# Index queries and keys held as high and low fp32r parts, their scores as three products on the two row halves

## The chip, the cores and the metric

The kernel runs on one core of one Trainium2 chip. The metric is the device time in microseconds (us) of one execution; the time before the change is the median of three runs. TensorE is PE in the profile (PEld are its weight loads), VectorE is DVE, ScalarE is ACT, GpSimd is POOL, and SyncE is SP. What one engine hands to another goes through counting semaphores: a producer increments one at the end of an instruction, and a consumer waits for a value.

## The reference

Two layers, each a half-step SwiGLU feed-forward network, a token mixing, and a second half-step network; 256 tokens, 1024 features, all in float32. The change touches the mixing, and in it the indexer: 8 index heads of width 64 score every key for every query, and the 64 best keys of each query are then attended to by 8 heads. Cut to what matters:

```python
proj = rms_norm(h) @ w_in                      # q_a, c_raw, q_i (8 x 64), k_i (64), w_i (8), qkv_f, f_logit
rel   = einsum('bqhd,bsd->bqhs', q_i, k_i) * 64**-0.5
score = einsum('bqh,bqhs->bqs', w_i * 8**-0.5, relu(rel))   # masked to keys not after the query
_, idx = top_k(score, 64)                      # which keys head group a attends to
```

Scores are computed in float32: a rounding error in them may change which key is the 64th.

## The kernel before, in words

Every large product is made of fp32r matmuls. A weight chunk arrives by DMA in `raw`; ACT casts it to its high part `whi`, DVE (in places POOL) subtracts to get the low part `wlo`; activations are split in the same way (`xhi`, `xlo`). A product of two split operands is three fp32r matmuls, high by high, high by low, low by high (`three`, L624; `wide`, L630, does two of them in one of 512 columns). Products of operands that are not split are done by TensorE in float32 directly; the trace shows such a matmul as two records, each with a weight load.

The order of the work is written out by hand, one program for each engine, and each engine runs its own strictly in that order. The start of a layer's mixing (`mix`) goes as follows.

On PE: the latent and the index key, with 80 columns (`first`, L921); the four tiles of index queries, `tile(QI)` to `tile(QI + 3)`, each 24 matmuls of 256 columns, two heads to a tile. Half way through the first tile the row scales are spread; half way through the second come small products for the gates and the latent's norm (`token_major`); half way through the third `latent_rows` spreads the latent's scales, which waits for `cdiag_out`. Then the running sum of the forget gates (L932, waits for `logf_out`), the fourth tile, and the index scores: `index(h2, bank)` for the four pairs of heads, among the keys' and values' products of the other heads. An index pair has head 0 on array rows 0 to 63 and head 1 on rows 64 to 127, each with its own PSUM bank: one matmul of 128 columns for each (L944), and one of 256 columns for each (L948), all in float32.

The tiles alternate between two PSUM banks (`GU + j % 2`), so tile j may start only once tile j - 2 has been read out: `tile` waits for `qi_out` at L814.

On ACT: `query_out(j)` (L473) copies a tile of queries from PSUM to `feat`; between these copies it casts the weight chunks (`front`, `back`), loads the tables for exp and ln, and computes `lz` from the gates (L488, L490).

On DVE: the low parts of the chunks (L1103, L1109), the index key (L1286, written twice, once for each row half), the gates (L1292 to L1300), the latent's mean square (`cms`, L1303), which POOL raises to the power -1/2 (`crstd`, L340, 1.61 us), the diagonal from it (`cdiag_out`, L1307), `logf` (L1310), the normed latent `cn` (L1313) and its low part (L1316). Then it weighs and sums the heads' scores (L1326) and takes the 64 largest in eight rounds, at whose end `drop` (L1345) marks the rest.

`ohi` and `olo` are the fp32r tiles of the attention's output (8 blocks of 128 x 256); until the attention's heads are done, at L1263 and L467, nothing is in them.

Of the kernel before, what the change touches and what calls it, by code (L numbers as in the profile page):

```python
# [17 lines left out]
F32 = mybir.dt.float32  # L18
F32R = mybir.dt.float32r
BF16 = mybir.dt.bfloat16  # L20
ALU = mybir.AluOpType
ACT = mybir.ActivationFunctionType

P = 128
D = 1024
S = 256
S3 = 3 * P
# [3 lines left out]
HD = 64  # L31
# [32 lines left out]
KI, QI, KA, QA, FX = 0, 1, 5, 9, 13  # L64
NFEAT = 21
NQI = KA - QI
NWIDE = 8
NTILE = 1 + NFEAT - QA - NWIDE
# [13 lines left out]
def trunk(nc, x, stream, final_gain, consts, rel_bias, out, table):  # L82
    with ExitStack() as ctx:
# [3 lines left out]
        def sems(names):  # L87
            return [ctx.enter_context(nc.semaphore(n)) for n in names.split()]
# [10 lines left out]
        rows = sb("rows", [P, S])  # L99
# [17 lines left out]
        feat = sb("feat", [P, NFEAT, S])  # L117
# [33 lines left out]
        ohi = sb("ohi", [P, KT, S], F32R)  # L151
        olo = sb("olo", [P, KT, S], F32R)
# [16 lines left out]
        ps = ctx.enter_context(nc.psum_tensor("ps", [P, 8, 512], F32))  # L169
        GU = 4  # L170
# [12 lines left out]
        NPAIR = NH  # L183
        TILEB = 5, 4, 3, 2
        tlo = [t[:, i, :] for t in (ur, ht) for i in range(2)]
        tsum = [val[:, i // 2, D // 2 + i % 2 * S:D // 2 + (i % 2 + 1) * S] for i in range(4)]


# [15 lines left out]
        gate_mm, glo_out, gsum_out, ulo_out, usum_out = sems("gate_mm glo_out gsum_out ulo_out usum_out")  # L204
        sig_out, hg_out, h_out, hhi_out, hlo_out, acc_mm = sems("sig_out hg_out h_out hhi_out hlo_out acc_mm")
        feat_mm, feat_out, ka_out, qi_out, wo_mm = sems("feat_mm feat_out ka_out qi_out wo_mm")
        tlo_out, tsum_out, scaled_out = sems("tlo_out tsum_out scaled_out")
        part_out, xg_out, fin_act = sems("part_out")[0], sems("xg_out0 xg_out1"), sems("fin_act")[0]
        ncum_out, ncum_in, decay_in, decay_set = sems("ncum_out ncum_in decay_in decay_set")
# [5 lines left out]
        idx_mm, relu_out, score_out, top_step, drop_out = sems("idx_mm relu_out score_out top_step drop_out")  # L215
# [152 lines left out]
        def _(act):  # L368
# [77 lines left out]
            def mix(l):  # L446
                def front(m):
                    split_front(l, NF + m, used=MIX_USED[m][0] if m < MIXC else FRONT)
# [20 lines left out]
                def query_out(j):  # L469


                    act.wait_ge(feat_mm, l * NFEAT + j + 1)
                    nc.scalar.copy(feat[:, j, :], ps[:, GU + j % 2, 0:S]).then_inc(qi_out, 1)  # L473

                if l == 0:
                    act.wait_ge(table_out, 32)
# [6 lines left out]
                query_out(QI)  # L483
                act.wait_ge(c_mm, l + 1)
                front(2)

                act.wait_ge(az_out, l + 1)
                nc.scalar.activation(ez[:], az[:], ACT.Exp, scale=-1.0).then_inc(ez_out, 1)  # L488
# [119 lines left out]
            n = DEPTH * 3  # L608
            for b in range(NB):
                for j in range(2):  # L610
                    at = slice(j * 512, (j + 1) * 512)
# [11 lines left out]
        def _(pe):  # L623
# [176 lines left out]
            def mix(l):  # L800
# [8 lines left out]
                def tile(j, s, at, midway=None, bank=GU):  # L809

                    if QI + 2 <= j < QA:
                        pe.wait_ge(qi_out, l * NQI + (j - 2))  # L814
                    elif j >= QA + NWIDE + 2:
                        pe.wait_ge(feat_out, l * NTILE + (j - QA - NWIDE))
                    elif j >= QA + NWIDE:
                        pe.wait_ge(tsum_out, l * NWIDE + (j - QA - 1))
                    for k in range(KT):
                        if midway and k == KT // 2:  # L820
                            midway()
                        t = three(ps[:, bank + j % 2, 0:S], w(s, at + k * P, P), xt(k), k == 0, k == KT - 1)
                    t.then_inc(feat_mm, 1)
# [92 lines left out]
                def latent_rows():  # L916
# [5 lines left out]
                t, u = first([(ps[:, CB, 0:S], lambda k: w(0, k * P, P)),  # L922
                              (ps[0:KW, KIB, 0:S], lambda k: w(0, KT * P + k * KW, KW))], l * (3 * KT) + KT)
# [7 lines left out]
                for b in range(NB):  # L931
                    t = nc.tensor.matmul(ps[0:NH, SUM, b * P:S], logf[:, b, :], tri[:, b, b * P:S], start=b == 0, stop=b == 1)  # L932
# [3 lines left out]

                def index(h2, bank):

                    pe.wait_ge(qi_out, l * NQI + (h2 + 1))
                    if h2 >= 2:  # L940
                        pe.wait_ge(relu_out, l * NH + 2 * (h2 - 1))
                    for i in range(2):
                        rows = slice(HD * i, HD * i + HD)
                        nc.tensor.matmul(ps[:, bank + i, 0:P], feat[rows, QI + h2, 0:P], feat[rows, KI, 0:P],  # L944
                                         start=True, stop=True)
                    for i in range(2):
                        rows = slice(HD * i, HD * i + HD)
                        nc.tensor.matmul(ps[:, bank + i, P:S3], feat[rows, QI + h2, P:S], feat[rows, KI, :],  # L948
                                         start=True, stop=True).then_inc(idx_mm, 1)

                pe.wait_ge(feat_out, l * NTILE + 1)
                pe.wait_ge(cn_out, l + 1)
                pe.wait_ge(z_out, l + 1)
                def key(j):

                    if j < KA + 2:
                        pe.wait_ge(qi_out, l * NQI + (j - 2))
                    else:
                        pe.wait_ge(ka_out, l * (QA - KA) + (j - KA - 1))
                    three(ps[:, GU + j % 2, 0:S], w(s, UNIT + (j - KA) * P, P), (chi[:, :], clo[:, :]),  # L960
                          True, True).then_inc(feat_mm, 1)
# [7 lines left out]
                for b in range(NB):  # L969
                    t = three(ps[:, b, :], (chi[:, b * P:(b + 1) * P], clo[:, b * P:(b + 1) * P]),  # L970
                              w(s, UNIT + 512, 512), True, True)
# [125 lines left out]
        def _(dve):  # L1097
# [123 lines left out]
            def mix(l):  # L1221
                def front(m, halves=(0, 1)):
                    split_front(l, NF + m, used=MIX_USED[m][0] if m < MIXC else FRONT, halves=halves)

                def back(m):
                    split_back(l, NF + m, used=MIX_USED[m][1] if m < MIXC else UNIT)
# [45 lines left out]
                def tile_sum(t):  # L1272

                    if t >= 4:
# [2 lines left out]
                    nc.vector.tensor_tensor(tsum[t % 4], ps[:, TILEB[t % 4], 0:S], tlo[t % 4], ALU.add  # L1277
                                            ).then_inc(tsum_out, 1)

                dve.wait_ge(const_in, 16)  # L1280
                dve.wait_ge(c_mm, l + 1)
                nc.vector.tensor_tensor(ct, ps[:, CB, 0:S], rows[:, :], ALU.mult).then_inc(ct_out, 1)
# [2 lines left out]
                for half in (slice(0, HD), slice(HD, P)):  # L1285
                    t = nc.vector.tensor_tensor(feat[half, KI, :], ps[0:HD, KIB, 0:S], rows[0:HD, :], ALU.mult)  # L1286
                t.then_inc(feat_out, 1)
                back(1)
                dve.wait_ge(wf_mm, l + 1)
                for b in range(NB):  # L1290
                    at = b * 2 * NH
# [9 lines left out]
                                               op1=ALU.max).then_inc(az_out, 1)  # L1301
                dve.wait_ge(css_mm, l + 1)
                nc.vector.tensor_scalar(cms[:, :], ps[:, CB, 0:NB], 1.0 / P, EPS, ALU.mult, ALU.add).then_inc(cms_out, 1)  # L1303
                front(2, (0,))
                dve.wait_ge(crstd_out, l + 1)
                for b in range(NB):
                    t = nc.vector.tensor_scalar(diag[:, b, :], ident, crstd[:, b:b + 1], None, ALU.mult)  # L1307
# [4 lines left out]
                dve.wait_ge(crows_mm, l + 1)  # L1312
                nc.vector.tensor_tensor(cn, ct, ps[:, CB, 0:S], ALU.mult).then_inc(cn_out, 1)  # L1313
                back(2)
                dve.wait_ge(chi_out, l + 1)
                nc.vector.scalar_tensor_tensor(out=clo[:], in0=cn, scalar=gains_all[:, l, G_CKV:G_CKV + 1],  # L1316
                                               in1=chi[:].bitcast(F32), op0=ALU.mult, op1=ALU.subtract
                                               ).then_inc(clo_out, 1)
                front(3)

                for h in range(NH):
                    dve.wait_ge(relu_out, l * NH + (h + 1))
# [216 lines left out]
```

## Time and profile before

| what | value |
|---|---|
| median of three runs | 1002.46 us (1002.4 to 1002.56) |
| the profiled execution | 1003.15 us |
| its span, first to last instruction | 1001.3 us |
| granted TensorE clock, mean | 0.998 of full speed |
| PE busy | 991.9 us, 99% of the span |
| DVE busy | 754.8 us, 75% |
| ACT busy | 538.8 us, 54% |
| POOL busy | 139.7 us, 14% |

The profiled execution is 0.69 us longer than the median, and its span is 1.85 us shorter than its own time. A matmul's duration in a row is its latency; in a stream of matmuls the distance from one start to the next is what one costs. A row of the timeline that says x4 is four records merged, with the time from the first start to the last end.

### The profile page before, as it was taken

To read this page: it belongs to the slowest core of one execution; us is meant where nothing else is said; L and a number is where in the kernel's file an instruction comes from. 1 tells how busy PE (TensorE), PEld (TensorE's weight loads), DVE (VectorE), ACT (ScalarE), POOL (GpSimd) and SP (SyncE) were. 2 spreads that over 40 slices of the span, in tenths; PEclk is the share of its full clock that TensorE was granted. 3 is DMA by queue.
4 is the path that set the end of the run, shared out by engine and by line. 5 is a ranking of instruction groups with operands and counts; after the bars stand their busy time and mean duration, and the time that the engine had idled before them with its cause. 6 is when DMAs were issued, how large, how long until landed. Compare 5 with 4: busy or idle time off the path is not lost.

```text
span 1001.3 us, 16517 instructions
## 1 busy us (share of the span) xinstructions
PE 991.9 (99%) x5647; PEld 844.6 (84%) x5647; DVE 754.8 (75%) x1503; ACT 538.8 (54%) x977; POOL 139.7 (14%) x154
## 2 busy tenths in 40 slices
PE   9999999999999999999999999999999999999997
PEld 8888888888878888888888888889887788888885
DVE  5887777679667887777788777777786688777775
ACT  5555555565565555555455555555755555555553
POOL 2000000018761000000000000000297500000001
PEclk9999999999999999999999999999999999999999
DMA  8665555765534665555536555554563446555541
GB/s 303 209 198 188 189 186 189 250 230 179 199 107 151 219 196 189 189 189 189 189 130 213 195 186 187 187 185 149 185 214 129 170 149 221 190 189 189 189 147 43
DMA packets 38021, 184.76 MB, mean 185 GB/s; under 512 B 3888, under 2 KB 8160, under 8 KB 23776
## 3 DMA queue, kind: packets, MB, share of 16 engines
q1 hardware_dynamic: 33264, 178.60, 53.7%
q10 hardware_dynamic: 4720, 5.67, 1.8%
q8 instruction: 23, 0.38, 0.2%
q14 instruction: 14, 0.11, 0.0%
HBM read 183.18 MB, written 2.64 MB: 186 GB/s over the span
## 4 chain that ended last, share of the span: by engine, by line
PE 98%; DMA 1%; DVE 0%; POOL 0%; DVEq 0%; issue 0%
PE ps L632 33%; PE ps L633 17%; PE ps L626 13%; PE ps L628 12%; PE ps L627 12%; PE ps L718 1%; PE ps L642 1%; PE ps L883 1%; PE ps L646 1%; PE ps L643 1%; PE ps L895 1%; PE ps L874 1%; PE ps L870 1%; DMA cst<-consts 1%; PE ps L728 0%; PE ps L899 0%
## 5 line engine op out<-in xcount | busy, mean ns | idle before, releaser
L632 PE MATMUL ps<-xboth,whi 128*128 128x512 f32 x1440 | 508.0, 395 | 0.0
L633 PE MATMUL ps<-xboth,wlo 128*128 128x256 f32 x1440 | 403.4, 280 | 0.0
L632 PEld LDWEIGHTS ps<-xboth,whi 128*128 128x128 f32 x1440 | 269.9, 187 | 63.7 <-issue 1.0
L633 PEld LDWEIGHTS ps<-xboth,wlo 128*128 128x128 f32 x1440 | 272.0, 189 | 3.6
L1103 DVE TENSOR_TENSOR wlo<-raw,whi 128x1024 fp32r<-128x1024 f32 (+1 forms) x214 | 250.3, 1206 | 6.0 <-ACT whi L373 6.0
L373 ACT CAST whi<-raw 128x1024 fp32r<-128x1024 f32 (+1 forms) x222 | 217.5, 1029 | 7.4 <-PE ps L628 7.4
L1109 DVE TENSOR_TENSOR wlo<-raw,whi 128x1024 fp32r<-128x1024 f32 (+1 forms) x110 | 132.8, 1207 | 99.9 <-ACT whi L377 99.8
L413 ACT ACTIVATE sig<-hg 128x256 f32<-128x256 f32 x88 | 36.9, 419 | 198.5 <-DVE hg L1181 182.4
L377 ACT CAST whi<-raw 128x1024 fp32r<-128x1024 f32 (+1 forms) x112 | 112.8, 1007 | 53.4 <-PE ps L628 53.0
L628 PE MATMUL ps<-whi,hlo 128*128 128x512 f32 x352 | 138.9, 395 | 0.0
L627 PE MATMUL ps<-wlo,hhi 128*128 128x512 f32 x352 | 138.8, 394 | 0.0
L626 PE MATMUL ps<-whi,hhi 128*128 128x512 f32 x352 | 138.6, 394 | 0.0
L285 POOL TENSOR_TENSOR rstd<-ms,mhalf 128x1 f32<-128x1 f32 x14 | 13.6, 983 | 591.8 <-DVE ms L1120 591.4
L418 ACT CAST hhi<-hf 128x256 fp32r<-128x256 f32 x88 | 35.8, 406 | 98.2 <-DVE hf L1198 98.2
L628 PEld LDWEIGHTS ps<-whi,hlo 128*128 128x128 f32 x352 | 66.3, 188 | 15.3
L626 PEld LDWEIGHTS ps<-whi,hhi 128*128 128x128 f32 x352 | 66.3, 188 | 15.1
L627 PEld LDWEIGHTS ps<-wlo,hhi 128*128 128x128 f32 x352 | 66.3, 188 | 11.8
L1200 DVE TENSOR_TENSOR hlo<-hf,hhi 128x256 fp32r<-128x256 f32 x88 | 37.4, 426 | 41.6 <-ACT hhi L418 41.6
L626 PE MATMUL ps<-xboth,whi 128*128 128x256 f32 x160 | 46.5, 291 | 0.0
L627 PE MATMUL ps<-xboth,whi 128*128 128x256 f32 x160 | 45.2, 283 | 0.0
L628 PE MATMUL ps<-xboth,wlo 128*128 128x256 f32 x160 | 45.2, 283 | 0.0
L1186 DVE TENSOR_TENSOR ht<-ur,sig 128x256 f32<-128x256 f32 x88 | 37.5, 426 | 9.2
(175 smaller groups left out, 1189.5 us busy)
## 6 DMA issues: line engine op xcount, KB each, us to landing
raw<-stream SPq DMA_DIRECT2D x111, 1024.0 KB, 5.2
raw<-stream SPq DMA_DIRECT2D x113, 512.0 KB, 3.6
decay<-table ACTq DMA_DIRECT2D x2, 1024.0 KB, 8.4
table<-table ACTq DMA_DIRECT2D x1, 1524.0 KB
X<-x SPq DMA_DIRECT2D x2, 512.0 KB, 5.6
bias<-table ACTq DMA_DIRECT2D x1, 1024.0 KB, 5.7
cst<-consts SPq DMA_DIRECT2D x1, 576.0 KB, 11.1
raw<-stream SPq DMA_DIRECT2D x2, 256.0 KB, 6.4
```

What stands on the lines that cost most here:

```text
L373: nc.scalar.copy(whi[:, k % 2, at], raw[:, k % 2, at]).then_inc(hi_front, 1)
L377: nc.scalar.copy(whi[:, k % 2, FRONT:FRONT + used], raw[:, k % 2, FRONT:FRONT + used]).then_inc(hi_back, 1)
L413: nc.scalar.activation(sig[:, s, :], hg[:, s, :], ACT.Sigmoid).then_inc(sig_out, 1)
L626: nc.tensor.matmul(out_, a[0], b[0], start=start, stop=False)
L627: nc.tensor.matmul(out_, a[0], b[1], start=False, stop=False)
L628: return nc.tensor.matmul(out_, a[1], b[0], start=False, stop=stop)
L632: nc.tensor.matmul(ps[:, bank, :], a[0], xboth[:, k, :], start=k == 0, stop=False)
L633: return nc.tensor.matmul(ps[:, bank, 0:S], a[1], xhi[:, k, :], start=False, stop=k == KT - 1)
L1103: nc.vector.tensor_tensor(wlo[:, s, at], raw[:, s, at], whi[:, s, at].bitcast(F32), ALU.subtract).then_inc(w_front, 1)
L1109: nc.vector.tensor_tensor(wlo[:, s, at], raw[:, s, at], whi[:, s, at].bitcast(F32), ALU.subtract).then_inc(w_back, 1)
L1186: nc.vector.tensor_tensor(ht[:, s, :], ur[:, s, :], sig[:, s, :], ALU.mult).then_inc(ht_out, 1)
L1200: nc.vector.tensor_tensor(hlo[:, s, :], hf[:, s, :], hhi[:, s, :].bitcast(F32), ALU.subtract).then_inc(hlo_out, 1)
```

## The change: split index operands

The index queries are no longer copied to `feat` as float32. ACT casts each tile from PSUM to a high part in `ohi[:, 0:4]`, and DVE subtracts that from the same PSUM tile to get the low part in `olo[:, 0:4]` (`query_low`). The index key gets a high part (ACT, from `feat`) in `ohi[:, 4]` and a low part (DVE) in `olo[:, 4]`. Each float32 matmul of `index` becomes three fp32r matmuls, written so that the two row halves alternate. PE's waits for `qi_out` become waits for `qi_lo_out`, since PSUM is free only when DVE too has read it.

```diff
@@ names
+        iq_hi, iq_lo = ohi[:, 0:NQI, :], olo[:, 0:NQI, :]
+        ik_hi, ik_lo = ohi[:, NQI, :], olo[:, NQI, :]
@@ ACT: query_out, and behind front(2)
-                    nc.scalar.copy(feat[:, j, :], ps[:, GU + j % 2, 0:S]).then_inc(qi_out, 1)
+                    nc.scalar.copy(iq_hi[:, j - QI, :], ps[:, GU + j % 2, 0:S]).then_inc(qi_out, 1)
...
+                act.wait_ge(feat_out, l * NTILE + 1)
+                nc.scalar.copy(ik_hi, feat[:, KI, :]).then_inc(ki_hi_out, 1)
@@ PE: tile, and key in the same way
-                        pe.wait_ge(qi_out, l * NQI + (j - 2))
+                        pe.wait_ge(qi_lo_out, l * NQI + (j - 2))
@@ PE: index
-                    pe.wait_ge(qi_out, l * NQI + (h2 + 1))
+                    pe.wait_ge(qi_lo_out, l * NQI + (h2 + 1))
...
-                    for i in range(2):
-                        rows = slice(HD * i, HD * i + HD)
-                        nc.tensor.matmul(ps[:, bank + i, 0:P], feat[rows, QI + h2, 0:P], feat[rows, KI, 0:P],
-                                         start=True, stop=True)
-                    for i in range(2):
-                        rows = slice(HD * i, HD * i + HD)
-                        nc.tensor.matmul(ps[:, bank + i, P:S3], feat[rows, QI + h2, P:S], feat[rows, KI, :],
-                                         start=True, stop=True).then_inc(idx_mm, 1)
-
-                pe.wait_ge(feat_out, l * NTILE + 1)
+                    for at, qs, n in ((slice(0, P), slice(0, P), P), (slice(P, S3), slice(P, S), S)):
+                        for q, key, start, stop in ((iq_hi, ik_hi, True, False), (iq_hi, ik_lo, False, False),
+                                                    (iq_lo, ik_hi, False, True)):
+                            for i in range(2):
+                                rows = slice(HD * i, HD * i + HD)
+                                t = nc.tensor.matmul(ps[:, bank + i, at], q[rows, h2, qs], key[rows, 0:n],
+                                                     start=start, stop=stop)
+                                if stop and n == S:
+                                    t.then_inc(idx_mm, 1)
+
+                pe.wait_ge(ki_lo_out, l + 1)
@@ DVE
+                def query_low(j):
+                    dve.wait_ge(qi_out, l * NQI + (j + 1))
+                    nc.vector.tensor_tensor(iq_lo[:, j, :], ps[:, GU + (QI + j) % 2, 0:S], iq_hi[:, j, :].bitcast(F32),
+                                            ALU.subtract).then_inc(qi_lo_out, 1)
...
                 back(1)
+                query_low(0)
                 dve.wait_ge(wf_mm, l + 1)
...
+                dve.wait_ge(feat_out, l * NTILE + 1)
+                dve.wait_ge(ki_hi_out, l + 1)
+                nc.vector.tensor_tensor(ik_lo, feat[:, KI, :], ik_hi.bitcast(F32), ALU.subtract).then_inc(ki_lo_out, 1)
                 front(2, (0,))
...
                 back(2)
+                query_low(1)
                 dve.wait_ge(chi_out, l + 1)
...
-                front(3)
+                query_low(2)
+                front(3, (0,))
+                query_low(3)
+                front(3, (1,))
```

Where the new work stands on DVE, from the low part of the first queries' chunk to the low part of the latent. Names are those of the tiles: `wlo<-raw,whi` is a chunk's low part, `hf<-hg,ps` is `cn`. Before:

```order
L1109 TENSOR_TENSOR wlo<-raw,whi 128x1024 [waits hi_back]
L1292 TENSOR_SCALAR wf<-ps,rstd 128x8 [waits wf_mm]
...
L1303 TENSOR_SCALAR cms<-ps 128x2 [waits css_mm]
L1103 TENSOR_TENSOR wlo<-raw,whi 128x1024 [waits hi_front]
L1307 TENSOR_SCALAR diag<-cst,crstd 128x128 [waits crstd_out]
...
L1310 TENSOR_TENSOR logf<-mz,lz 128x16 [waits lz_out]
L1103 TENSOR_TENSOR wlo<-raw,whi 128x1024 [waits hi_front]
L1313 TENSOR_TENSOR hf<-hg,ps 128x256 [waits crows_mm]
L1109 TENSOR_TENSOR wlo<-raw,whi 128x1024 [waits hi_back]
L1316 SCALAR_TENSOR_TENSOR clo<-hf,cst,chi 128x256 [waits chi_out]
```

And now, with the same names (`olo<-ps,ohi` is `query_low`, `olo<-feat,ohi` the key's low part):

```order
L1115 TENSOR_TENSOR wlo<-raw,whi 128x1024 [waits hi_back]
L1288 TENSOR_TENSOR olo<-ps,ohi 128x256 [waits qi_out]
L1304 TENSOR_SCALAR wf<-ps,rstd 128x8 [waits wf_mm]
...
L1315 TENSOR_SCALAR cms<-ps 128x2 [waits css_mm]
L1318 TENSOR_TENSOR olo<-feat,ohi 128x256 [waits ki_hi_out,feat_out]
L1109 TENSOR_TENSOR wlo<-raw,whi 128x1024 [waits hi_front]
L1322 TENSOR_SCALAR diag<-cst,crstd 128x128 [waits crstd_out]
...
L1325 TENSOR_TENSOR logf<-mz,lz 128x16 [waits lz_out]
L1109 TENSOR_TENSOR wlo<-raw,whi 128x1024 [waits hi_front]
L1328 TENSOR_TENSOR hf<-hg,ps 128x256 [waits crows_mm]
L1115 TENSOR_TENSOR wlo<-raw,whi 128x1024 [waits hi_back]
L1288 TENSOR_TENSOR olo<-ps,ohi 128x256 [waits qi_out]
L1332 SCALAR_TENSOR_TENSOR clo<-hf,cst,chi 128x256 [waits chi_out]
```

One subtraction now stands ahead of the gates and `cms`, one between `cms` and the chunk's low part, and one ahead of the latent's low part.

On PE the first index pair of a layer; before, with the second pair behind it:

```order
L944 MATMUL ps<-feat 128x128 [waits z_out,qi_out,cn_out,feat_out]
L944 MATMUL ps<-feat 128x128
L948 MATMUL ps<-feat 128x256 x2
L944 MATMUL ps<-feat 128x128 [waits qi_out]
L944 MATMUL ps<-feat 128x128
L948 MATMUL ps<-feat 128x256 x2
```

And now the first pair alone (`ps<-ohi` is high by high):

```order
L952 MATMUL ps<-ohi 128x128 [waits z_out,qi_lo_out,cn_out,ki_lo_out]
L952 MATMUL ps<-ohi 128x128
L952 MATMUL ps<-olo,ohi 128x128 x2
L952 MATMUL ps<-ohi,olo 128x128 x2
L952 MATMUL ps<-ohi 128x256 x2
L952 MATMUL ps<-olo,ohi 128x256 x2
L952 MATMUL ps<-ohi,olo 128x256 x2
```

Four float32 matmuls of a pair of heads have become twelve fp32r ones, at the same place.

## Rows read from the trace of the kernel before

**Rows 1.** Page, part 1: busy time, share of the span, instructions.
```profile
PE 991.9 (99%) x5647; PEld 844.6 (84%) x5647; DVE 754.8 (75%) x1503; ACT 538.8 (54%) x977; POOL 139.7 (14%) x154
```
**Rows 2.** Page, part 4: the chain that ended last, by engine.
```profile
PE 98%; DMA 1%; DVE 0%; POOL 0%; DVEq 0%; issue 0%
```
**Rows 3.** Timeline of PE: start, us, operation, idle before; first layer's first index pairs.
```profile
219.16 0.60 PE L948 MATMUL ps<-feat 64*128 64x256 f32 x4
219.59 0.39 PE L944 MATMUL ps<-feat 64*128 64x128 f32 x4
219.81 0.60 PE L948 MATMUL ps<-feat 64*128 64x256 f32 x4
```
**Rows 4.** Groups of PE by form: all narrow index matmuls' records.
```profile
L944 PE MATMUL ps<-feat 64*128 64x128 f32 x32 | 3.7, 310 | 0.0
```
**Rows 5.** Timeline of PE: fp32r matmuls of 256 columns in a query tile.
```profile
210.62 0.28 PE L628 MATMUL ps<-xboth,wlo 128*128 128x256 f32 x1
210.74 0.28 PE L626 MATMUL ps<-xboth,whi 128*128 128x256 f32 x1
```
**Rows 6.** Timeline of PEld: weight loads of four one-column matmul records.
```profile
209.47 0.52 PEld L912 LDWEIGHTS ps<-ones,sig 128*128 128x128 f32 x4
```
**Rows 7.** Timeline of DVE, first layer, index key to latent.
```profile
208.42 1.23 DVE L1109 TENSOR_TENSOR wlo<-raw,whi 128x1024 fp32r<-128x1024 f32 x1
209.59 0.28 DVE L1292 TENSOR_SCALAR wf<-ps,rstd 128x8 f32<-128x8 f32 x1
...
210.54 0.15 DVE L1303 TENSOR_SCALAR cms<-ps 128x2 f32<-128x2 f32 x1
210.61 1.21 DVE L1103 TENSOR_TENSOR wlo<-raw,whi 128x1024 fp32r<-128x1024 f32 x1
212.41 0.48 DVE L1307 TENSOR_SCALAR diag<-cst,crstd 128x128 f32<-128x128 f32 x2 [0.59 <-POOL crstd L340]
...
213.05 1.22 DVE L1103 TENSOR_TENSOR wlo<-raw,whi 128x1024 fp32r<-128x1024 f32 x1
214.18 0.42 DVE L1313 TENSOR_TENSOR hf<-hg,ps 128x256 f32<-128x256 f32 x1
214.51 1.22 DVE L1109 TENSOR_TENSOR wlo<-raw,whi 128x1024 fp32r<-128x1024 f32 x1
```
**Rows 8.** One line of DVE: a low part subtracted from PSUM.
```profile
L1263 DVE TENSOR_TENSOR olo<-ps,ohi x16: 414/420/425, 265.2 to 802.9; 128x256 fp32r<-128x256 f32 x16
```
**Rows 9.** Timeline of POOL, first layer.
```profile
210.77 1.61 POOL L340 TENSOR_TENSOR crstd<-cms,mhalf 128x2 f32<-128x2 f32 x1 [6.80 <-DVE cms L1303]
```
**Rows 10.** Timeline of PE, first layer, around the spread and the fourth tile.
```profile
212.78 0.28 PE L628 MATMUL ps<-xboth,wlo 128*128 128x256 f32 x1
212.95 0.71 PE L728 MATMUL ps<-diag,ones 128*128 128x128 f32 x4
...
215.77 0.39 PE L626 MATMUL ps<-xboth,whi 128*128 128x256 f32 x1
```
**Rows 11.** Timeline of ACT, first layer: tables, `lz`, a query tile.
```profile
209.88 1.28 ACT L488 ACT_TABLE_LOAD   x1
...
212.71 0.21 ACT L490 ACTIVATE lz<-ez 128x16 f32<-128x16 f32 x1
...
213.76 0.37 ACT L473 COPY feat<-ps 128x256 f32<-128x256 f32 x1
```
**Rows 12.** Page, part 5: ACT's cast of a 128x256 tile.
```profile
L418 ACT CAST hhi<-hf 128x256 fp32r<-128x256 f32 x88 | 35.8, 406 | 98.2 <-DVE hf L1198 98.2
```
**Rows 13.** Timeline of DVE: the end of the first layer's selection.
```profile
244.49 1.01 DVE L1345 SCALAR_TENSOR_TENSOR drop<-score,cst 128x384 bf16<-128x384 f32 x1
```
**Rows 14.** Timeline of PE: its first use of the selection.
```profile
247.65 0.50 PE L867 MATMUL ps<-drop,nident 128*128 128x384 bf16 x2
```
**Rows 15.** Timeline of DVE, second layer: the same diagonal.
```profile
704.54 0.48 DVE L1307 TENSOR_SCALAR diag<-cst,crstd 128x128 f32<-128x128 f32 x2 [0.59 <-POOL crstd L340]
```
**Rows 16.** Timeline of PE, second layer: the same spread.
```profile
705.08 0.71 PE L728 MATMUL ps<-diag,ones 128*128 128x128 f32 x4
```

More of the change, by code:

```diff
@@ L206, in trunk @@
         feat_mm, feat_out, ka_out, qi_out, wo_mm = sems("feat_mm feat_out ka_out qi_out wo_mm")
+        qi_lo_out, ki_hi_out, ki_lo_out = sems("qi_lo_out ki_hi_out ki_lo_out")
         tlo_out, tsum_out, scaled_out = sems("tlo_out tsum_out scaled_out")
@@ L956, in key @@
                     if j < KA + 2:
-                        pe.wait_ge(qi_out, l * NQI + (j - 2))
+                        pe.wait_ge(qi_lo_out, l * NQI + (j - 2))
                     else:
```

## The prediction, written before the result was known

> **What bounds the kernel now.** I read the page first: PE is busy 991.9 of 1001.3 us, DVE 754.8 [rows 1], and the chain that ended last is PE for 98% [rows 2]. So TensorE's time and every moment in which TensorE is made to wait go into the result one for one; work added to ACT, DVE or POOL costs only where PE waits for it. Then the timeline of each engine in the stretch that the change touches, 204 to 226 us, and again at 700 to 720 us, since there are two layers. The reader is to look there for two things: what the index matmuls cost as a stream, start to start, and how long before PE asks for it each result of DVE and ACT is ready.
>
> **The matmuls.** Before, an index pair streams a narrow and a wide part. The narrow part runs from 219.59 to 219.81, the wide one from 219.16 to the next narrow one at 219.59 [rows 3]: 0.22 + 0.43 = 0.65 us. The narrow row holds four records: two float32 matmuls of two passes each, the two row halves side by side, 0.11 a pass; the wide passes are 0.215 each. There are 32 narrow records in all [rows 4], so 8 pairs.
>
> Now a pair is 3 narrow and 3 wide steps, each step both row halves. A wide fp32r step: consecutive fp32r matmuls of 256 columns start 0.12 us apart [rows 5], so 3 x 0.12 = 0.36. A narrow fp32r matmul is nowhere in this trace. From below: half of a 256-column one, 0.06. From above: what float32 costs for 128 columns, both passes, 0.22 [rows 3]. I take 0.11, because the loads set that pace: before one-column matmuls, with nothing to stream, four loads of 128 columns take 0.52 us, and with the last one's own 0.19 (the duration of a load in such a row) off, the three steps between them are (0.52 - 0.19)/3 = 0.11 [rows 6]. Every narrow matmul brings its own load of 128 columns, so a shorter stream would not help. Sum: 3 x 0.11 + 0.36 = 0.69 instead of 0.65: +0.04 a pair, 8 pairs, **+0.3 us**. Thus cutting float32's passes by a quarter in columns saves nothing here, because narrow steps fill up with loads. That the two halves go side by side in fp32r as in float32 I take from the same rows.
>
> The trace's 0.11 us agrees with a rule of the Trainium skill, "TensorE: Matmul & The Clock Gate", section "LDWEIGHTS (loading the stationary operand)": the columns loaded divided by 1.2 give the ns, so 107 ns for 128. By the same page's "Back-to-back issue gap", though, a stream of load and matmul pairs sustains 81 ns at 128 columns; by that, an estimate, the 24 narrow steps would cost 0.7 us less and the sum come out at 1003.5 us.
>
> **The first wait: the latent's scales.** PE spreads them at 212.95, where DVE's diagonal ends (212.41 + 0.48 = 212.89) [rows 7, 10]. PE itself could have begun at 212.78 + 0.12 = 212.90, so there is no reserve to speak of: 0.05 us. The diagonal waited for POOL (0.59 idle ahead of it), POOL's 1.61 us run off `cms` at 210.54 [rows 7, 9]. The first `query_low` now stands ahead of `cms`. Its duration is that of the same operation on the attention's output, 0.42 [rows 8], but instructions overlap: the PSUM read at 214.18 was followed at 214.51, 0.33 later [rows 7]. Between 0.33 and 0.42 I take 0.35. `cms`, POOL, diagonal and spread all move by it: PE +0.35. The key's low part, behind `cms`, costs about as much again but falls into the 0.59 idle ahead of the diagonal: 0.35 + 0.35 of DVE work behind a POOL result that is itself 0.35 later leaves 0.24 of it. If that cover were too short, the excess would be added to the wait.
>
> **The second wait: the fourth query tile.** PE starts it at 215.77 [rows 10]. It needs the second tile's PSUM bank free. Before, that was ACT's copy, done at 213.76 + 0.37 = 214.13 [rows 11], 1.6 us early. Now it is `query_low(1)`, which stands behind `back(2)` on DVE. I follow DVE: `logf` needs ACT's `lz`, and ACT now casts the key (0.41 long, [rows 12], some 0.32 start to start) ahead of the first table load at 209.88 [rows 11]; the whole of what follows, `lz` too, is 0.32 later: 212.92 becomes 213.24. The diagonal ends at 213.25, so both arrive together, and the chunk's half after `logf` starts at 213.05 + 0.32 = 213.37. With the distances of before, 1.13 to `cn`, 0.33 to `back(2)` [rows 7], it is 214.83; 1.17 later (208.42 to 209.59 is that distance [rows 7]) `query_low(1)` starts at 216.00 and ends at 216.42. With 0.05 to PE, as from diagonal to spread, that is 216.47. PE, already 0.35 late, would have been ready at 216.12: another +0.35. Together **+0.70 us** a layer. Queued behind this wait on PE are the fourth tile and all that follows, so nothing fills it. The bounds of the two waits together: 0.55 (each piece at its shortest, the 0.33) and 0.95 (each subtraction 0.42, the cast 0.41, and some 0.1 for PE's queue to fill again after it ran dry).
>
> The other three new waits are early. The key's low part is done by 211.4, the third tile's low part at 218.4 (clo's place moves to 217.5), the fourth's at 220.5, and PE asks for them at 219.5, 221.1 and 221.5 in its shifted time.
>
> **Further on.** DVE has 5 x 0.35 to 0.42 = 1.8 to 2.1 us more work in this stretch. The one consumer far behind is the selection: `drop` ends at 244.49 + 1.01 = 245.50, and PE takes it at 247.65 [rows 13, 14], 2.15 us of cover, while PE itself comes later. So it costs nothing; without that cover PE would pay up to 1.3 us a layer. The second layer repeats the first: its diagonal ends at 704.54 + 0.48 = 705.02 and the spread starts at 705.08 [rows 15, 16]. ACT's casts to fp32r instead of copies change nothing on a path. No DMA is added.
>
> **Sum.** 2 x 0.70 + 0.3 = 1.7 us. The profiled execution of 1003.15 us would become 1004.85; the median of the runs is 0.7 below the profiled one, so 1002.46 + 1.7 = **1004.2 us**. About 0.2%, 2.0 us, is what a measurement can tell from no change, so this counts as no change, near its upper edge of 1004.46. With the bounds of its terms (waits 2 x 0.55 to 2 x 0.95, matmuls 0.1 to 0.5) the forecast's own range is 1003.7 to 1004.9.
>
> **The rivals.** *Narrow fp32r runs at float32's pace.* Every fp32r matmul of before has 256 columns or more, none has 128, and that can be because narrow ones are slow: 0.22 a step instead of 0.11, 24 steps, +2.6: 1006.8 us, slower. It decides as soon as a narrow step takes over 0.12 us, since 0.26 us more in all crosses 1004.46. Against it: the only thing in the rows that holds a narrow step up is the load, and that is 0.11. Chance 0.16.
>
> *The halves don't overlap.* Twelve steps of fp32r one after the other, 0.69 more a pair: +5.5, 1009.7 us. For it: the two halves now accumulate over three matmuls; against it: they write separate banks and did overlap in float32 [rows 3]. Chance 0.05.
>
> *Narrow steps are cheap.* A load of 64 rows is hidden, and the step costs 0.06: 24 x 0.05 = 1.2 less, 1003.0 us. The loads in [rows 6] are of 128 rows, which leaves room for it. Chance 0.12. It is what the skill's "TensorE: Matmul & The Clock Gate" gives for an isolated gap (128/2.4 + 2.5 = 56 ns); by that rule the trace's 0.11 would not be a floor.
>
> *The change does not slow PE's waits as I say:* DVE's and ACT's order has more play than I read, and only the matmuls' 0.3 us remains, 1002.8 us. For it: each wait rests on a few tenths. Against it: [rows 7, 9 and 10] show the first chain without play. With part of the waits, or with cheap narrow steps as well (1001.6), it is still within 0.2%. Chance 0.15. For a result faster by over 0.2%, PE would have to save over 2 us; the pair's floor, 3 x 0.06 + 0.36 = 0.54 against 0.65, gives 0.9 in all.
>
> **The numbers.** The forecast has 0.52. Slower: 0.16 + 0.05 and about a third of the forecast's own range, that above 1004.46, 0.18, so 0.39. Faster 0.03, for a mechanism that I don't see. Within 0.2% the rest, 0.58. The range from 1002.8 to 1006.9 leaves out the serial halves, some of the slow narrow case and a few hundredths below.
>
> **What would show it.** In the profile after: an index pair of 0.69 us, its narrow steps 0.11 apart; the spread some 0.35 us later against the tile before it, with DVE's diagonal ending just ahead; the fourth tile's first load right behind `query_low(1)`; the selection still two us early. I am wrong if narrow steps are 0.2 apart, if the two row halves start one after the other, or if PE does not stand before the fourth tile.

## The result and the profile after

The changed kernel takes 1004.85 us, median of 12 runs (1004.68 to 1005.49), beside 1002.62 us for the kernel before on the same chip (12 runs, 1002.31 to 1003.17). The ratio is 1.0022, with a 95% interval of 1.0014 to 1.0030: 2.2 us more, clear of no change, though the interval leaves open on which side of 0.2% it lies. The time is 0.65 us above the forecast, inside the range and just inside the forecast's own range, which ended at 1004.9.

The profiled execution took 1004.78 us, its span is 1003.0 us at a granted clock of 0.998. The page's busy times and its chain, which answer to [rows 1, 2]:

```profile
PE 992.4 (99%) x5679; PEld 845.8 (84%) x5679; DVE 756.9 (75%) x1513; ACT 539.5 (54%) x979; POOL 138.3 (14%) x154
...
PE 97%; DVE 1%; ACT 1%; DMA 0%; issue 0%; POOL 0%; DVEq 0%
```

PE is busy 0.5 us more while the span grew by 1.7. DVE and ACT now have a per cent each in the chain: PE stands somewhere and waits for them. One group of part 5 of the page says where (busy us and mean ns, then the idle time ahead and its releaser):

```profile
L631 PE MATMUL ps<-xboth,whi 128*128 128x256 f32 x160 | 46.5, 290 | 1.5 <-DVE olo L1288 1.5
```

1.5 us of idle over two layers, released by DVE's line 1288, which is `query_low`. The timeline of PE at that place, first and second layer (start, us; what [rows 10, 16] show of before):

```profile
212.13 0.28 PE L633 MATMUL ps<-xboth,wlo 128*128 128x256 f32 x1
212.25 0.71 PE L733 MATMUL ps<-diag,ones 128*128 128x128 f32 x4
...
214.32 0.82 PE L937 MATMUL ps<-cst,logf 128*8 128x256 f32 x4
215.88 0.36 PE L631 MATMUL ps<-xboth,whi 128*128 128x256 f32 x1 [0.74 <-DVE olo L1288]
...
707.64 0.82 PE L937 MATMUL ps<-cst,logf 128*8 128x256 f32 x4
709.18 0.35 PE L631 MATMUL ps<-xboth,whi 128*128 128x256 f32 x1 [0.72 <-DVE olo L1288]
```

Absolute times of the two traces don't compare: this execution began 0.65 us shorter, at its first transposes, and keeps that up to 212.13, where the row of before stands at 212.78 [rows 10]. So 0.65 is added below wherever a time of after is put beside one of before. The spread: 212.25 + 0.65 = 212.90 instead of 212.95, no later. The fourth tile: from the matmuls of `logf` to its first one it was 215.77 [rows 10] - 215.03 = 0.74 us, now 215.88 - 214.32 = 1.56. The row of before:

```profile
215.03 0.82 PE L932 MATMUL ps<-cst,logf 128*8 128x256 f32 x4
```

DVE, from the first `query_low` to the second, beside [rows 7]:

```profile
208.91 0.42 DVE L1288 TENSOR_TENSOR olo<-ps,ohi 128x256 fp32r<-128x256 f32 x1
...
210.19 0.15 DVE L1315 TENSOR_SCALAR cms<-ps 128x2 f32<-128x2 f32 x1
210.25 0.41 DVE L1318 TENSOR_TENSOR olo<-feat,ohi 128x256 fp32r<-128x256 f32 x1
210.59 1.22 DVE L1109 TENSOR_TENSOR wlo<-raw,whi 128x1024 fp32r<-128x1024 f32 x1
211.72 0.47 DVE L1322 TENSOR_SCALAR diag<-cst,crstd 128x128 f32<-128x128 f32 x2
212.62 0.18 DVE L1325 TENSOR_TENSOR logf<-mz,lz 128x16 f32<-128x16 f32 x1 [0.42 <-ACT lz L495]
...
215.32 0.41 DVE L1288 TENSOR_TENSOR olo<-ps,ohi 128x256 fp32r<-128x256 f32 x1
```

The diagonal no longer waits for POOL; `logf` waits for ACT instead, 0.42 us; and the second `query_low` ends at 215.73, 0.15 ahead of PE's fourth tile. POOL's scale, beside [rows 9], takes half the time:

```profile
210.41 0.81 POOL L343 TENSOR_TENSOR crstd<-cms,mhalf 128x2 f32<-128x2 f32 x1 [7.08 <-DVE cms L1315]
```

The index pair in PE's timeline, beside [rows 3] (x2 are the two row halves, which start 3 ns apart):

```profile
219.71 0.22 PE L952 MATMUL ps<-ohi 64*128 64x128 f32 x2
219.77 0.28 PE L952 MATMUL ps<-olo,ohi 64*128 64x128 f32 x2
219.88 0.27 PE L952 MATMUL ps<-ohi,olo 64*128 64x128 f32 x2
220.00 0.33 PE L952 MATMUL ps<-ohi 64*128 64x256 f32 x2
220.16 0.28 PE L952 MATMUL ps<-olo,ohi 64*128 64x256 f32 x2
220.28 0.28 PE L952 MATMUL ps<-ohi,olo 64*128 64x256 f32 x2
```

From 219.71 to 220.28 + 0.12 it is 0.69 us. The steps are not even: the first narrow one is followed after 0.06 us, the other two after 0.11, and the first wide one after 0.16.

The rest was found by setting each matmul of one trace beside the same one of the other and following the lag, by how much later it starts. From the first layer's mixing on it changes at four places a layer; the first figure is of the first layer, the second of the other:

| where the lag grows | us | forecast, a layer |
|---|---|---|
| spread of the latent's scales | -0.06, -0.05 | +0.35 |
| fourth query tile | +0.78, +0.76 | +0.35 |
| four index pairs | +0.14, +0.14 | +0.16 |
| 64 pairs of wide and narrow matmuls behind the last index pair | +0.33, +0.34 | 0 |

The sum is 1.19 a layer, 2.38 in all, against 2.23 between the medians and 2.38 - 0.65 = 1.7 between the spans. The last line was not in the forecast. Behind the last index pair, for 20 us, PE runs the wide projection as pairs of a 512-column and a 256-column matmul. Nine pairs in before and in after (timeline of PE, the 512-column rows):

```profile
226.06 0.39 PE L632 MATMUL ps<-xboth,whi 128*128 128x512 f32 x1
...
229.18 0.39 PE L632 MATMUL ps<-xboth,whi 128*128 128x512 f32 x1
```

```profile
226.29 0.40 PE L637 MATMUL ps<-xboth,whi 128*128 128x512 f32 x1
...
229.47 0.40 PE L637 MATMUL ps<-xboth,whi 128*128 128x512 f32 x1
```

3.12 us and 3.18: 346.7 ns a pair in before, 353.3 in after, by the unrounded starts. Nothing is idle in either and the instructions are the same; the later stream of such pairs in the feed-forward part runs at 349.7 ns on average in both kernels. Over the whole stretch the 6.6 ns make +0.42, less 0.09 for a small hold-up at the 25th pair (433 ns instead of 347) that before has and after hasn't. Now the question was which part of the change sets that pace, and whether the 0.78 is made as the forecast says.

### The profile page after: what moved, and what is told of

The parts are those of the page before. It is cut to its first block, busy times and chain, and to the rows that moved or that the text cites. A ratio compares the mean times of both kernels' runs of the same rounds, so it can differ in the third digit from the quotient of the medians.

```text
span 1003.0 us, 16595 instructions
## 1 busy us (share of the span) xinstructions
PE 992.4 (99%) x5679; PEld 845.8 (84%) x5679; DVE 756.9 (75%) x1513; ACT 539.5 (54%) x979; POOL 138.3 (14%) x154
## 4 chain that ended last, share of the span: by engine, by line
PE 97%; DVE 1%; ACT 1%; DMA 0%; issue 0%; POOL 0%; DVEq 0%
PE ps L637 33%; PE ps L638 17%; PE ps L631 13%; PE ps L633 12%; PE ps L632 12%; PE ps L647 1%; PE ps L723 1%; PE ps L888 1%; PE ps L651 1%; PE ps L648 1%; PE ps L900 1%; PE ps L879 1%; PE ps L875 1%; PE ps L952 1%; DMA cst<-consts 0%
```

## Experiments

Each was timed beside the kernel before on the same chip: experiments 1 to 4 on one chip (median of before 1002.62 us), 5 to 8 on a second (1002.68), 9 to 12 on a third (1002.87). Experiments 7 and 12 are one run each, without a ratio. "Pace" is ns per pair in the stretch above, alike in both layers every time.

**1. Everything but the fp32r products.** The index matmuls of after read the high parts as float32; casts, subtractions and waits stay.

```diff
+ nc.tensor.matmul(ps[:, bank + i, 0:P], iq_hi[rows, h2, 0:P].bitcast(F32), ik_hi[rows, 0:P].bitcast(F32),
+                  start=True, stop=True)      # and P:S3 likewise
- (the three fp32r products)
```

> The changed kernel with the index products back in float32 (one matmul each, four for a pair of heads), taken from the high parts alone; the casts, the subtractions and all new waits stay. It leaves the low parts out of the scores, so it selects by rounded scores. Theory: the change costs three separate things, each once a layer: a wait ahead of the fourth query tile (0.70 us against the kernel before), the index pairs (4 x 0.04 = 0.14), and a slower cadence of the wide tiles that follow (0.32), which comes from how the fp32r index pairs leave TensorE. Then this kernel keeps only the wait: 1.4 us over before, 1004.0, and in the trace its wide tiles run at 347 ns for a pair of a wide and a narrow matmul, as before. Rival: the slower cadence comes from the extra work on DVE and ACT or from where the stretch lies in time; then the wide tiles stay at 353 ns and the time is about 1004.7.

Measured 1004.08 us, ratio 1.0014 (1.0005 to 1.0023). Pace 346.7: the waits, casts and subtractions don't set it. The lag has the fourth tile's +0.77 in both layers and the -0.05 at the spread, and nothing else.

```profile
214.82 0.82 PE L937 MATMUL ps<-cst,logf 128*8 128x256 f32 x4
216.36 0.35 PE L631 MATMUL ps<-xboth,whi 128*128 128x256 f32 x1 [0.72 <-DVE olo L1287]
...
226.27 0.40 PE L637 MATMUL ps<-xboth,whi 128*128 128x512 f32 x1
...
229.39 0.39 PE L637 MATMUL ps<-xboth,whi 128*128 128x512 f32 x1
```

**2. Only the fp32r products.** The kernel before, its query and key written as fp32r, twelve products a pair, all of high parts.

```diff
- nc.scalar.copy(feat[:, j, :], ...)        + nc.scalar.copy(iq_hi[:, j - QI, :], ...)
+ for q, key, start, stop in ((iq_hi, ik_hi, True, False), (iq_hi, ik_hi, False, False), (iq_hi, ik_hi, False, True)):
```

> The kernel before with only the twelve fp32r products of a pair of heads: high parts alone (each of the three products is high by high), queries cast by ACT where it copied them, the key cast by DVE in the instruction that wrote it; no subtraction, no new wait. It leaves the low parts out of the scores. Theory: 8 x 0.04 = 0.3 us for the pairs and 2 x 0.32 = 0.64 for the cadence of 353 instead of 347 ns a pair of matmuls: 1003.5 us, and PE starts the fourth tile without a wait, as before. Rival (cadence set by DVE, ACT or the wait): 347 ns, and 1002.9 us.

Measured 1003.49 us, ratio 1.0009 (0.9999 to 1.0018). The lag: pairs +0.13 and +0.14, wide pairs +0.32 and +0.33, no wait.

```profile
226.01 0.40 PE L633 MATMUL ps<-xboth,whi 128*128 128x512 f32 x1
...
229.19 0.40 PE L633 MATMUL ps<-xboth,whi 128*128 128x512 f32 x1
```

3.18 us for nine pairs. So the slower pace comes with the products, the wait with the rest, and experiments 1 and 2 together give the whole: 1.46 + 0.87 = 2.33 us beside the change's 2.23.

**3. The second `query_low` ahead of `back(2)`.**

```diff
- back(2)
- query_low(1)
+ query_low(1)
+ back(2)
```

> The changed kernel with the second subtraction of queries ahead of the chunk's low part on DVE (query_low(1), then back(2)) instead of behind it. Theory: the wait ahead of the fourth tile goes as a whole, since the subtraction now ends about 0.5 us before PE has finished the sum of the gates: 0.74 us a layer, 1004.85 - 1.5 = 1003.4 us, and no other wait comes in its place (the fourth tile's own low part is ready about 0.9 us early, the chunk's low part about 9 us). Rival: a later wait, for query_low(3) or for the chunk, takes it back, and the time stays above 1004.2 us.

Measured 1003.23 us, ratio 1.0005 (0.9996 to 1.0014). Against the matmuls of `logf` the subtraction starts 1.14 us earlier (0.14 ahead of them instead of 1.00 behind; it now stands ahead of the 1.2 us one), and PE's step to the fourth tile is 0.75, as in before:

```profile
214.69 0.82 PE L937 MATMUL ps<-cst,logf 128*8 128x256 f32 x4
215.44 0.39 PE L631 MATMUL ps<-xboth,whi 128*128 128x256 f32 x1
```

```profile
214.55 0.41 DVE L1288 TENSOR_TENSOR olo<-ps,ohi 128x256 fp32r<-128x256 f32 x1
214.88 1.21 DVE L1115 TENSOR_TENSOR wlo<-raw,whi 128x1024 fp32r<-128x1024 f32 x1
```

The wait was the order on DVE, and swapping two calls removes it. The pace stayed at 353.3.

**4. The key's cast and subtraction late.** The changed kernel, but ACT casts the key only behind `lz`, and DVE subtracts only behind the second `query_low`.

```diff
  nc.scalar.activation(... lz ...)
+ nc.scalar.copy(ik_hi, feat[:, KI, :])       # stood ahead of the tables
...
  query_low(1)
+ nc.vector.tensor_tensor(ik_lo, feat[:, KI, :], ik_hi.bitcast(F32), ALU.subtract)   # stood behind cms
```

> The changed kernel with the key's high part cast by ACT behind lz instead of ahead of the tables, and its low part subtracted behind query_low(1). Theory one, lz alone decides: lz is 0.32 us earlier, and the fourth tile's wait shrinks from 0.74 to about 0.4 us: 1004.2 us. Theory two, POOL's power takes 0.81 us where it starts ahead of a long SBUF subtraction of DVE and 1.61 where it starts under one: with the key's subtraction no longer between cms and the chunk, POOL takes 1.6 us again, the diagonal is some 0.35 us later, logf with it, and the wait stays near 0.7 us: 1004.8 us.

Measured 1004.46 us, ratio 1.0018 (1.0008 to 1.0028), between what the two theories gave. POOL, DVE and PE:

```profile
210.81 1.61 POOL L343 TENSOR_TENSOR crstd<-cms,mhalf 128x2 f32<-128x2 f32 x1 [7.09 <-DVE cms L1315]
```

```profile
210.65 1.21 DVE L1109 TENSOR_TENSOR wlo<-raw,whi 128x1024 fp32r<-128x1024 f32 x1
212.46 0.48 DVE L1319 TENSOR_SCALAR diag<-cst,crstd 128x128 f32<-128x128 f32 x2 [0.59 <-POOL crstd L343]
```

```profile
215.07 0.82 PE L937 MATMUL ps<-cst,logf 128*8 128x256 f32 x4
216.10 0.36 PE L631 MATMUL ps<-xboth,whi 128*128 128x256 f32 x1 [0.22 <-DVE olo L1288]
```

With the key's subtraction gone from behind `cms`, POOL is back at 1.61 us and the diagonal waits its 0.59 again. Now the lag is +0.29 and +0.28 at the spread and +0.26 and +0.27 at the fourth tile: the forecast's first wait does appear, once POOL takes what the forecast took. The fourth tile's share falls from 0.78 to 0.27 because about half of the delay was already paid at the spread, and the total from 0.72 to 0.55: in before's time `logf` is now 0.15 us late instead of 0.31.

**5. The last index pair in float32**, on top of experiment 3. The theory: the matmul that stands right ahead of the stream sets its pace.

```diff
+ if h2 == 3:    # products in float32 from the high parts, then return
```

> The kernel of e4 (second subtraction moved ahead) with the products of the last pair of index heads alone in float32, from the high parts; it leaves the low parts out of that pair's scores. Theory: the cadence of the wide tiles is set by what TensorE did right before them, so with a float32 pair there it is 347 ns for a wide and a narrow matmul, and the time 0.64 + 0.07 us under e4: 1002.5 us. Rival: it is set by the number of fp32r index products or by what came further back; 353 ns stays, and the time is 1003.2 us.

Measured 1003.21 us, ratio 1.0006 (0.9996 to 1.0015), pace still 353.4. The theory falls. The entry is even that of before, in which four float32 matmuls stand ahead too: the first two intervals between wide matmuls are 453 and 351 ns (452 and 352 in before), and only the third goes apart, 360 against 347.

```profile
225.99 0.40 PE L637 MATMUL ps<-xboth,whi 128*128 128x512 f32 x1
...
229.17 0.40 PE L637 MATMUL ps<-xboth,whi 128*128 128x512 f32 x1
```

**6 and 7. A matmul of no use ahead of the first wide pair**, on top of experiment 3: float32 on 64 rows with 128 columns, then fp32r on 128 rows with 256 columns.

```diff
+ if t == 0:   # 6
+     nc.tensor.matmul(ps[:, TILEB[0], 0:P], ident[0:HD, :], ident[0:HD, :], start=True, stop=True)
+ if t == 0:   # 7
+     nc.tensor.matmul(ps[:, TILEB[0], 0:S], chi[:, 0:P], chi[:, :], start=True, stop=True)
```

> The kernel of e4 with one needless float32 matmul on row half 0 (128 columns) right ahead of the first wide tile of each layer. Theory (what was there last sets the cadence): 347 ns a pair of matmuls, 0.64 us less, and 2 x 0.2 to 0.4 us more for the dummy with its two passes: 1002.8 to 1003.4 us. Rival (the index products themselves set it): 353 ns, 1003.7 to 1004.0 us.

> The kernel of e4 with one needless fp32r matmul of full rows and 256 columns right ahead of the first wide tile. If it is float32 that sets the fast cadence, this one leaves 353 ns. If any change of the moment at which the stream of wide tiles begins can flip it, 347 ns is as likely. It costs 2 x 0.12 to 0.2 us.

The float32 one: 1003.78 us, ratio 1.0013 (1.0003 to 1.0023), pace 353.3, so the theory missed. The fp32r one: pace 346.7, 1002.88 us in its one run.

**8. Narrow products widened to 256 columns**, the key's whole width for every one, to see whether a narrow step is bound by its load.

```diff
- for at, qs, n in ((slice(0, P), slice(0, P), P), (slice(P, S3), slice(P, S), S)):
+ for at, qs, n in ((slice(0, S), slice(0, P), S), (slice(P, S3), slice(P, S), S)):
```

> The changed kernel with the three narrow index products of a pair widened from 128 to 256 columns; the surplus is overwritten by the wide ones. Theory: a narrow step costs 0.11 us because its weight load takes that, so 256 columns cost hardly more (0.117 against 0.11 to 0.115): 24 x 0.005 = 0.1 us, 1004.95 us. Rival: narrow steps are bound by their columns or by the issue of instructions with some overlap; then each gets 0.05 us longer, 24 x 0.05 = 1.2 us: 1006.0 us.

Measured 1005.09 us, ratio 1.0024 (1.0014 to 1.0034). By the lag the four pairs of a layer cost 0.10 us more than in after.

```profile
219.94 0.28 PE L952 MATMUL ps<-ohi 64*128 64x256 f32 x2
220.06 0.28 PE L952 MATMUL ps<-olo,ohi 64*128 64x256 f32 x2
...
220.54 0.28 PE L952 MATMUL ps<-ohi,olo 64*128 64x256 f32 x2
```

Six steps of 0.12 are 0.72 where 0.69 stood: twice the columns cost some 0.01 us a step, so the columns are not what a narrow step waits for, as the forecast said. That it is the load is not shown apart from this: the loads too start 0.11 us apart, but any other fixed cost of a step would look the same.

**9. Experiment 7, timed.** Both remedies at once: the call moved and the fp32r matmul put in.

> The kernel of f5b, timed: the second subtraction ahead of the chunk's low part, and one needless fp32r matmul of 256 columns ahead of the first wide tile. Theory: the sum of what the change costs is waits (2 x 0.70), pairs (2 x 0.14) and cadence (2 x 0.32); this kernel takes the first and the last back and pays 2 x 0.1 for the dummy: 1002.68 + 0.28 + 0.2 - 2 x 0.07 for the first wait of before, 1003.0 us, or down to 1002.6 if the dummy lies beside something. Rival: the one look of f5b was a low one and the cadence is worth nothing: 1003.4 us.

Measured 1002.74 us beside 1002.87, ratio 0.9999 (0.9990 to 1.0008): the times can't tell it from the kernel before. By the lag it still is some 0.2 us longer, about what the index pairs cost, so the waits and the slow pace are gone and nothing is gained over the kernel before.

```profile
225.99 0.39 PE L637 MATMUL ps<-xboth,whi 128*128 128x512 f32 x1
...
229.11 0.39 PE L637 MATMUL ps<-xboth,whi 128*128 128x512 f32 x1
```

**10. The same fp32r matmul in the kernel before**, whose pace is the quick one without it.

> The kernel before with the same needless fp32r matmul ahead of the first wide tile. If an fp32r matmul of full rows there sets the fast cadence by itself, the wide tiles stay at 347 ns and the time is 1002.68 + 0.2 = 1002.9 us. If it only shifts the moment at which the stream starts, and which cadence follows is a matter of that, it may as well turn to 353 ns: 1003.5 us.

Measured 1003.68 us, ratio 1.0007 (0.9997 to 1.0016), and the pace is slow:

```profile
226.05 0.40 PE L632 MATMUL ps<-xboth,whi 128*128 128x512 f32 x1
...
229.23 0.40 PE L632 MATMUL ps<-xboth,whi 128*128 128x512 f32 x1
```

What made one kernel quick makes the other slow. So such a matmul is no remedy in itself. Nor do the fp32r index products set the pace alone: this kernel has none of them and is slow, experiment 9 has all of them and is quick.

**11. A subtraction of no use in the kernel before**, between `cms` and the long one, where after has the key's.

```diff
+ nc.vector.tensor_tensor(olo[:, NQI, :], feat[:, KI, :], rows[:, :], ALU.subtract)
```

> The kernel before with one needless subtraction of 128 x 256 on DVE between cms and the chunk's low part, where the change puts the key's. Theory (POOL's power is held up by a long SBUF subtraction of DVE that starts ahead of it): POOL takes 0.81 instead of 1.61 us, the diagonal no longer waits for it, and PE's spread starts without the 0.07 us of before: 1002.5 to 1002.7 us though DVE does more. Rival: POOL takes 1.61 us as before, and the spread stays where it is or comes later: 1002.7 to 1003.3 us.

Measured 1002.55 us beside 1002.87, ratio 0.9996 (0.9986 to 1.0005), which the times alone can't tell from no change. The traces can: POOL takes 0.81, and from the last matmul ahead of the spread to the tile's next one behind it PE takes 213.16 - 212.67 = 0.49 us instead of 0.64 (212.78 [rows 10] to 213.42, the last row here).

```profile
210.66 0.81 POOL L340 TENSOR_TENSOR crstd<-cms,mhalf 128x2 f32<-128x2 f32 x1 [6.79 <-DVE cms L1303]
```

```profile
212.67 0.28 PE L628 MATMUL ps<-xboth,wlo 128*128 128x256 f32 x1
212.79 0.61 PE L728 MATMUL ps<-diag,ones 128*128 128x128 f32 x4
213.16 0.36 PE L626 MATMUL ps<-xboth,whi 128*128 128x256 f32 x1
```

```profile
213.42 0.36 PE L626 MATMUL ps<-xboth,whi 128*128 128x256 f32 x1
```

**12. The matmul of experiment 7 with 128 columns**.

> The kernel of e4 with a needless fp32r matmul of full rows and 128 columns, instead of 256, ahead of the first wide tile. If an fp32r matmul of full rows there sets the fast cadence, 347 ns; if its length matters, 353 ns.

Pace 353.5, 1003.93 us in its one run. The same rows and the same precision as in 7, fewer columns, and the pace doesn't turn. The two programs have the same instructions at the same places, so neither their number nor their place sets it.

## Why the prediction came out as it did

**The matmuls: right.** A pair was to take 0.69 us and does; a lag of 0.14 a layer is 0.035 a pair instead of 0.04. Its three rivals are refuted: a narrow fp32r step takes 0.11 us at most, not 0.22, the halves start 3 ns apart, and the narrow step isn't cheap, since doubling its columns hardly moves it (experiment 8).

**The waits: the sum right, the split wrong.** 0.70 a layer was forecast, 0.72 came (0.78 - 0.06), within the bounds; in before's time the second `query_low` ends at 215.73 + 0.65 = 216.38 (forecast 216.42) and the fourth tile starts at 216.53 (forecast 216.47). But the first half was not paid at the spread. The step that failed is "`cms`, POOL, diagonal and spread all move by it: PE +0.35". `cms` did move: it stands at 210.19 + 0.65 = 210.84 in before's time, 0.30 late. POOL's step did not keep its 1.61: it took 0.81, ending 0.56 us after the DVE subtraction under which it ran, which now is the key's short one (210.25 + 0.41 = 210.66, POOL ends 211.22) and was the long one (210.61 + 1.21 = 211.82, POOL ends 212.38) [rows 7, 9]. Experiment 4 takes the short one away and 1.61 comes back; experiment 11 puts one in before and gets 0.81. That POOL's duration goes by what DVE runs beside it is shown; why it does is not. The Trainium skill has a rule that bears on it, in "SBUF — State Buffer", section "SBUF: two separate sides", and the forecast did not use it: VectorE, in an operation with two SBUF inputs, and a GpSimd operation that reads SBUF contend for a shared pair of ports, an exclusive lock; whichever starts first holds it for its whole instruction, and the other blocks. The traces agree in that POOL ends 0.56 us past the subtraction under which it starts. They don't show the rest of the rule: DVE's long subtraction, which has two SBUF inputs and starts at 210.59, ran at the same time as POOL from 210.66 to 211.22, and neither held the other up: it took its usual 1.22 us.

The sum survived because the second path carried the full delay by itself: ACT's cast of the key makes `lz` 0.32 later (212.37 + 0.22 + 0.65 = 213.24, the forecast's figure to the hundredth), `logf`, the chunk, `cn`, `back(2)` and the second `query_low` follow in order, and the fourth tile waits for the last. The forecast had noted that the diagonal and `lz` arrive together; with two arrivals at once, the loss of one changes nothing behind them. So the sum came out partly by luck: of its two terms of 0.35 one was not paid where it was put, and the other was paid twice over. Experiment 3 shows the last link of the second path: one place earlier in DVE's queue, and the wait is gone. Experiment 4 bears on the first: with the cast behind `lz`, `logf` no longer waits for ACT and is half as late, though that kernel moves the key's subtraction as well. Experiment 11 has POOL's short step without the cast, and there `logf` stands where before has it and the fourth tile doesn't wait.

**What was missing: +0.33 a layer in the pace of the wide pairs.** No term of the sum stood for it, and the instructions there are unchanged. By the lag it is 0.67 us in all. The result lies 0.65 us above the forecast; 0.16 of that is the kernel before itself, whose median was 1002.62 here and 1002.46 where the forecast took it, and the rest is the sum's, 2.23 measured against 1.7, which this missing term more than fills. Without it the changed kernel would take some 1004.2 us (an estimate: 1004.85 - 0.67). Shown is that in this kernel it comes with the fp32r products (experiments 1 and 2), that it is not set by whether float32 ends the index stream (5, 6), nor by a full-row fp32r matmul as such (7, 10 and 12), nor by whether the index products are in fp32r (9 and 10), and that two values occur in this stretch and no third:

| pace | kernels |
|---|---|
| 346.7 to 346.8 ns | before; experiments 1, 7 and 9 (one kernel), 11 |
| 353.3 to 353.5 ns | after; experiments 2, 3, 4, 5, 6, 8, 10, 12 |

Before's interval alternates 230 and 117 ns; after's run through a longer cycle: 232, 118, 241, 120, 236, 113. That each kernel keeps its pace for the whole stretch, and has the same one in both layers, fits a pattern of loads and matmuls that is set by how the stream is entered and then repeats itself. That is argued, not shown. What in the entry sets it stays open; experiment 5 and before enter within 2 ns of each other over the first two intervals and take different paces.

**The rest: right.** The selection keeps its cover: `drop` and PE's first use of it in after, beside [rows 13, 14]:

```profile
244.93 0.74 DVE L1364 SCALAR_TENSOR_TENSOR drop<-score,cst 128x384 bf16<-128x384 f32 x1
```

```profile
248.19 0.50 PE L872 MATMUL ps<-drop,nident 128*128 128x384 bf16 x2
```

248.19 - 245.67 leaves 2.5 us. None of the other new waits shows idle time on PE, and the rival in which the waits don't arise is refuted by the 1.5 us.

## What to carry to other kernels

When an operand's producer is made longer, look for the last thing that PE waits for behind it and for its place in that engine's queue: here one 0.4 us subtraction behind a 1.2 us one cost 1.5 us over two layers, and swapping them gave it back. A short instruction on an engine that isn't the bottleneck may be priced by its neighbour on another engine; read such a duration with what ran beside it before it is carried over to a new order. And after a change compare the pace of the unchanged streams behind it: 2% on 64 pairs was more than twice what the changed matmuls themselves cost.

## What the runs showed of the hardware that was not expected

- The same fp32r stream of loads and matmuls runs at 346.7 or 353.3 ns a pair for 20 us, with no idle time in either. One extra matmul ahead of it turned the slow pace into the quick one in one kernel and the quick into the slow in another (experiments 7 and 10).
- POOL's operation on 128x2 elements takes 0.81 or 1.61 us, 0.56 past the end of the DVE subtraction beside it. One more DVE instruction, in the right place, let PE go on 0.16 us earlier a layer (experiment 11).
- The matmuls of one fp32r step on the two row halves start 3 ns apart, and a step costs 0.11 us at 128 columns and 0.12 at 256, so three products of 128 columns cost more than one float32 matmul of that size, 0.33 against 0.22 us.
